# A streaming encoder step whose last output projection is computed in rows of frames

## The reference, cut to what matters

```python
SEQ, DEC_SEQ, D_MODEL, D_FF = 512, 32, 1024, 2816     # 544 frames in all
def rms_norm(x, g):
    y = xf * lax.rsqrt(jnp.mean(xf * xf, axis=-1, keepdims=True) + EPS)
    return (y * g).astype(x.dtype)
def swiglu(h, w_in, w_out):
    gu = h @ w_in
    return (jax.nn.silu(gu[..., :D_FF]) * gu[..., D_FF:]) @ w_out
for layer in range(2):
    xp = rms_norm(hp, g[0]);  mp = mixer(xp)            # layer 0: gating + attention, layer 1: pooling
    hp = hp + rms_norm(mp, g[1])
    hp = hp + rms_norm(swiglu(rms_norm(hp, g[2]), ffn_w_in[layer], ffn_w_out[layer]), g[3])
```

## Time and profile before

| | us |
|---|---|
| median of 3 runs | 1025.32 (1025.29 to 1025.61) |
| the profiled execution's own time | 1024.44 |
| its span in the trace | 1022.6 |
| PE busy | 1009.1 (99%) |
| DVE busy | 628.7 (61%) |
| ACT busy | 523.5 (51%) |
| POOL busy | 47.4 (5%) |
| HBM read | 157.46 MB, 157 GB/s over the span |

### The profile page before, as it was taken

One profiled execution on the slowest core, in us unless ns is written; L12 is line 12 of the kernel. 1 busy time (PEld: TensorE's weight loads), 2 busy tenths in 40 slices (PEclk: granted clock), 3 DMA queues, 4 the chain that ended last, 5 costly groups with the idle time before them and its releaser, 6 DMA issues.

```text
span 1022.6 us, 19108 instructions
## 1 busy us (share of the span) xinstructions
PE 1009.1 (99%) x7908; PEld 991.7 (97%) x7908; DVE 628.7 (61%) x928; ACT 523.5 (51%) x919; POOL 47.4 (5%) x55
## 2 busy tenths in 40 slices
PE   7999999999999999999999999999999999999997
PEld 6799899999999999999999999999999999999997
DVE  5396555877555555545479777899655555444643
ACT  6633666555444444444457665775544444444552
POOL 0081210000000000000000000001000000000000
PEclk9999999999999999999999999999999999999999
DMA  8322131666665555546654586556655555555554
GB/s 281 84 76 79 55 97 51 188 191 184 187 183 169 165 165 165 166 131 184 183 168 145 156 218 175 161 168 190 184 166 165 166 164 150 154 164 163 155 166 148
DMA packets 307431, 161.29 MB, mean 158 GB/s; under 512 B 14666, under 2 KB 304306, under 8 KB 307344
## 3 DMA queue, kind: packets, MB, share of 16 engines
q1 hardware_dynamic: 306880, 159.61, 53.8%
q0 software_dynamic: 224, 0.35, 0.1%
q10 hardware_dynamic: 240, 0.10, 0.0%
HBM read 157.46 MB, written 2.58 MB: 157 GB/s over the span
## 4 chain that ended last, share of the span: by engine, by line
PE 90%; DVE 6%; ACT 2%; issue 1%; DMA 1%; SPq 0%; DVEq 0%; ACTq 0%
PE ps L556 29%; PE ps L558 28%; PE ps L557 28%; DVE wlo L1528 2%; DVE tmp L1804 1%; DMA x_tok<-in_x_prompt_dram 1%; PE ps L823 1%; PE ps L809 1%; PE ps L753 0%; PE ps L644 0%; DVE acc L1764 0%; ACT whi L1085 0%; PE ps L735 0%; DVE odd_a L1922 0%; DMA raw<-in_ffn_w_out_dram 0%
## 5 line engine op out<-in xcount | busy, mean ns | idle before, releaser
L1528 DVE TENSOR_TENSOR wlo<-raw,whi 128x1024 fp32r<-128x1024 f32 (+2 forms) x332 | 367.8, 1110 | 259.8 <-ACT whi L1085 259.6
L556 PE MATMUL ps<-xhi,whi 128*128 128x256 f32 (+1 forms) x1600 | 466.6, 292 | 0.7 <-DVE wlo L1528 0.5
L558 PE MATMUL ps<-xhi,wlo 128*128 128x256 f32 (+1 forms) x1600 | 460.8, 288 | 0.0
L557 PE MATMUL ps<-xlo,whi 128*128 128x256 f32 (+1 forms) x1600 | 459.9, 287 | 0.0
L1085 ACT ACTIVATE whi<-raw 128x1024 fp32r<-128x1024 f32 (+2 forms) x332 | 316.0, 954 | 225.7 <-PE ps L558 194.3
L556 PEld LDWEIGHTS ps<-xhi,whi 128*128 128x128 f32 x1600 | 300.9, 188 | 3.2 <-issue 1.3
L557 PEld LDWEIGHTS ps<-xlo,whi 128*128 128x128 f32 x1600 | 301.1, 188 | 0.0
L558 PEld LDWEIGHTS ps<-xhi,wlo 128*128 128x128 f32 x1600 | 300.9, 188 | 0.0
L556 PE MATMUL ps<-mhi_b,whi 128*128 128x288 f32 x352 | 104.7, 297 | 0.0
L558 PE MATMUL ps<-mhi_b,wlo 128*128 128x288 f32 x352 | 104.3, 296 | 0.0
L557 PE MATMUL ps<-mlo_b,whi 128*128 128x288 f32 x352 | 102.7, 292 | 0.0
(11 more groups left out here) (231 smaller groups left out, 901.6 us busy)
## 6 DMA issues: line engine op xcount, KB each, us to landing
raw<-in_ffn_w_in_dram SPq DMA_DIRECT2D x176, 512.0 KB, 3.9
raw<-in_ffn_w_out_dram SPq DMA_DIRECT2D x64, 384.0 KB, 3.2
raw<-in_ffn_w_out_dram SPq DMA_DIRECT2D x64, 320.0 KB, 2.9
raw<-in_ab_w_in_dram SPq DMA_DIRECT2D x10, 512.0 KB, 4.7
raw<-in_ab_w_out_dram SPq DMA_DIRECT2D x10, 256.0 KB, 2.8
raw<-in_ab_w_out_dram SPq DMA_DIRECT2D x20, 128.0 KB, 3.2
x_tok<-in_x_prompt_dram SPq DMA_DIRECT2D x4, 512.0 KB, 7.8
raw<-in_ab_w_in_dram SPq DMA_DIRECT2D x8, 256.0 KB, 4.1
```

What stands on the lines that cost most here:

```text
L556: pe.matmul(out, wh, xh, start=first, stop=False)
L557: pe.matmul(out, wh, xl, start=False, stop=False)
L558: return pe.matmul(out, wl, xh, start=False, stop=last)
L1528: dve.tensor_tensor(wlo[:, s, 0:n], raw[:, m % NRAW, 0:n], whi[:, s, 0:n].bitcast(F32), ALU.subtract)\
```

## The change

**The last pass.** `ffn_out(1, 0)` becomes `rows_out`. Now 128 frames of `mhi`/`mlo` sit in the array and 512 weight columns stream, so that the result stands in rows of frames. The pass has 22 units of 2 chunks by 512 columns (each 1024 columns, 512 KB): 11 for the left half of the features, 11 for the right. In each unit PE makes 6 products for frames 0 to 127 and 6 for frames 128 to 255. The last two units are reordered: both for the first frames, then both for the second.

**The post-norm.** ACT squares each [128, 512] piece with a running sum along the row (`accum_out`), so no matmul adds squares. DVE multiplies by the gain, which lies along the row now (`g_row`, 512 KB loaded by a broadcast at unit 8). The left half's two pieces are squared and scaled at slot 11, the right half's at the end; then one root, one inversion and two multiply-adds for each 128 frames. `turn_z`, `sums_last`, the two filler matmuls and the last block's own evacuation are gone. The side work of the pass has new slots.

**The spreads.** `spread` and `spread_first` now use transposes of the broadcast column instead of matmuls with the identity; the third tile of part 1 is spread at full width and overwritten where the second belongs.

**The start.** The first half of `turn_first(1)` moves from before `va_block(0, 0)` to after it, so all 8 transposes of tile 1 stand together.

```diff
-TURN_BEFORE = {(0, 1): (1, (1,)), (1, 0): (2,), (0, 2): (3,), (0, 3): (4,)}
+TURN_BEFORE = {(0, 1): (1,), (1, 0): (2,), (0, 2): (3,), (0, 3): (4,)}
...
-    (3, 1): {"sum": 1, "spread": 2, "scale": (2, 4, 6, 8), "rows": (11, 11, 13, 13, 15, 15)},
-    (3, 0): {"h_rows": (2, 3, 5, 6), "z_rows": (18, 19), "z_more": 29},
+    (3, 1): {"sum": 1, "spread": 2, "scale": (2, 3, 4, 6), "rows": (8, 8, 9, 9, 10, 10)},
+    (3, 0): {"h_rows": (2, 3, 4, 5), "half": 11, "load": 8},
...
+FO_UNITS = {(layer, b): FC if (layer, b) == (1, 0) else 4 * KC for layer in range(2) for b in range(2)}
...
+                elif unit[0] == "fo" and unit[1:3] == (1, 0):
+                    half, i = divmod(unit[3], FC // 2)
+                    src = ffn_w_out[1].rearrange("(c p) n -> p c n", p=P)[:, 2 * i:2 * i + 2, 512 * half:512 * (half + 1)]
+                    dst = tiles(m).rearrange("p (c n) -> p c n", c=2)
...
+                if UNITS[m] == ("fo", 1, 0, STAGE[3, 0]["load"]):
+                    sp.wait_ge(w_used, FO_PASS[1, 1][-1] + 1)
+                    sp.dma_start(g_row[:, :], norm_g[1, 3].partition_broadcast(P)).then_inc(g_row_loaded, 16)
...
-            for half in range(2):
-                for t in range(2):
-                    sp.wait_ge(y_ready[t], half + 1)
-                    cols = slice(512 * half, 512 * (half + 1))
+            for t in range(2):
+                for n, cols in enumerate((slice(0, 512), slice(512, 1024))):
+                    sp.wait_ge(y_ready[t], n + 1)
...
-                    lhs, rhs = rstd[0:w, t:t + 1].broadcast_to([w, P]), ident[0:w, 0:w]
-                    mm = pe.matmul(flat(6, P + t0, w), lhs, rhs, start=True, stop=True)
+                    mm = pe.transpose(flat(6, P + t0, w), rstd[0:w, t:t + 1].broadcast_to([w, P]), ident[0:w, 0:w])
...
-            turn_first(1, (0,))
...
-                for i, t in enumerate(POOL_ROWS[b]):
+                for i, t in reversed(tuple(enumerate(POOL_ROWS[b]))):
                     w = TILES[t][1]
-                    lhs = rs[:, 3 * b + i:3 * b + i + 1].broadcast_to([P, P])
-                    mm = pe.matmul(flat(6 + b, P + i * P, w), lhs, ident[:, P - w:P], start=True, stop=True)
+                    factor = rs[:, 3 * b + i:3 * b + i + 1].broadcast_to([P, P])
+                    mm = pe.transpose(flat(6 + b, (i + 1) * P - (P - w), P), factor, ident[:, :])
...
-            def turn_z(t, ds):
-
-                for d in ds:
-                    mm = pe.transpose(flat(4 * (d // 4) + t, d % 4 * P, P), z[:, d, t * P:(t + 1) * P], ident[:, :])
-                return mm
-
-            def sums_last(squares, first):
-
-                for i in range(2):
-                    mm = pe.matmul(flat(6 + i, 0, 1), squares[:, i * P:(i + 1) * P], ones[:, :], start=first, stop=not first)
-                return mm
+            def rows_out(run):
+
+                pe.wait_ge(up_mult, inner(1, 1, FC - 1) + 1)
+                pe.wait_ge(m_lo, inner(1, 0, FC - 1) + 1)
+
+                def unit(m, t):
+                    half, i = divmod(UNITS[m][3], FC // 2)
+                    s, rows = m % NSPLIT, slice(t * P, (t + 1) * P)
+                    for c in range(2):
+                        w = slice(512 * c, 512 * (c + 1))
+                        mm = product(flat((2, 0)[half] + t, 0, 512), mhi[0][:, 2 * i + c, rows], mlo[0][:, 2 * i + c, rows],
+                                     whi[:, s, w], wlo[:, s, w], i + c == 0, 2 * i + c == FC - 1)
+                    return mm
+
+                for slot, m in enumerate(FO_PASS[1, 0]):
+                    n = UNITS[m][3]
+                    pe.wait_ge(w_lo, m + 1)
+                    if n == FC // 2:
+                        pe.wait_ge(h_rows_kept, 4)
+                    if n < FC - 2:
+                        for t in range(2):
+                            mm = unit(m, t)
+                        mm.then_inc(w_used, 1)
+                    elif n == FC - 2:
+                        unit(m, 0)
+                    else:
+                        unit(m, 0).then_inc(rows_done, 1)
+                        unit(m - 1, 1)
+                        unit(m, 1).then_inc(rows_done, 1)
+                    run(slot)
...
-                for t, slot in enumerate(STAGE[3, 0]["z_rows"]):
-                    yield slot
-                    pe.wait_ge(h_rows_kept, 4)
-                    pe.wait_ge(z_out[0], z_count(3, 3))
-                    turn_z(t, range(4)).then_inc(z_rows_turned, 1)
-                yield STAGE[3, 0]["z_more"]
-                pe.wait_ge(z_out[0], z_count(3, 6))
-                pe.wait_ge(y_ready[3], 2)
-                pe.wait_ge(y_ready[4], 2)
-                for t in range(2):
-                    turn_z(t, range(4, 7))
-                pe.wait_ge(z_added[0], add_count(3, KC - 2))
-                pe.wait_ge(rstd_done[0], 6)
-                sums_last(acc[:, 0, :], True)
...
-            ffn_out(1, 0, stepper(last_half()))
-            pe.wait_ge(r_kept[1], KEPT[3, 0])
-            fill(FILL_TAIL, 2)
-            pe.wait_ge(z_out[0], z_count(3, KC - 1))
-            sums_last(tmp2[:, (KC - 1) % 2, :], False).then_inc(sq_summed[0], 1)
-            pe.wait_ge(z_last, 1)
-            for t in range(2):
-                turn_z(t, range(7, 8)).then_inc(z_rows_turned, 1)
+            rows_out(stepper(last_half()))
...
-            def evacuate_last(d):
-
-                src = flat(out_bank(1, 0, d), 0, CUT)
-                act.wait_ge(z_added[0], add_count(3, d - 2))
-                act.activation(tmp2[:, d % 2, frames(0)], src, ACT.Square).then_inc(z_out[0], 1)
-                act.activation(z[:, d, frames(0)], src, ACT.Copy, scale=gain(1, 3, d)).then_inc(z_last, 1)
+            def square_rows(half, t):
+
+                n = 2 * half + t
+                if half:
+                    act.wait_ge(rows_done, t + 1)
+                else:
+                    act.wait_ge(w_used, AT["fo", 1, 0, FC // 2 - 1] + 1)
+                    act.wait_ge(z_added[1], add_count(3, KC - 1))
+                act.activation(tmp2[:, t, 0:512], flat((2, 0)[half] + t, 0, 512), ACT.Square,
+                               accum_out=row_sq[:, n:n + 1]).then_inc(rows_squared, 1)
+
+            def root_rows(t):
+
+                act.wait_ge(rows_squared, 3 + t)
+                act.wait_ge(rows_biased, 1)
+                act.activation(ms[:, t:t + 1], row_sq[:, 2 + t:3 + t], ACT.Sqrt, scale=1.0 / D,
+                               bias=row_bias[:, t:t + 1]).then_inc(rooted[0], 1)
+
+            def rows_out(run):
+
+                for slot, m in enumerate(FO_PASS[1, 0]):
+                    run(slot)
+                    if m + 4 < len(UNITS):
+                        hi_part(m + 4)
+                    run(slot + LATER)
...
+                yield STAGE[3, 0]["half"]
+                square_rows(0, 0)
+                square_rows(0, 1)
...
-            act.wait_ge(sq_summed[0], stat_count(3, 0))
-            act.activation(ms[:, 0:2].unsqueeze(2), ps[:, 6 * 512:8 * 512].rearrange("p (k n) -> p k n", k=2)[:, :, 0:1], ACT.Sqrt, bias=eps[:, :]).then_inc(rooted[0], 1)
+            rows_out(stepper(last_half()))
+            for t in range(2):
+                square_rows(1, t)
+                root_rows(t)
...
-            invert(3, 0, 0)
-            dve.wait_ge(rstd_done[0], stat_count(3, 0))
-            dve.wait_ge(h_rows_kept, 4)
-            for half in range(2):
-                for t in range(2):
-                    dve.wait_ge(z_rows_turned, 2 * half + t + 1)
+            def scale_rows(half, t):
+
+                cols = slice(512 * half, 512 * (half + 1))
+                dve.wait_ge(rows_squared, 2 * half + t + 1)
+                dve.wait_ge(g_row_loaded, 16)
+                dve.tensor_tensor(z_rows[:, t, cols], flat((2, 0)[half] + t, 0, 512), g_row[:, cols], ALU.mult)\
+                    .then_inc(z_rows_scaled, 1)
+
+            def last_half():
+
+                yield from norms(3, 1, 0)
+                yield STAGE[3, 0]["half"]
+                scale_rows(0, 0)
+                scale_rows(0, 1)
+                dve.tensor_scalar(row_bias[:, :], row_sq[:, 0:2], 1.0 / D, EPS, ALU.mult, ALU.add).then_inc(rows_biased, 1)
+
+            def rows_out(run):
+
+                for slot, m in enumerate(FO_PASS[1, 0]):
+                    run(slot)
+                    if m + 4 < len(UNITS):
+                        lo_part(m + 4)
+
+            rows_out(stepper(last_half()))
+            for t in range(2):
+                scale_rows(1, t)
+                dve.wait_ge(rooted[0], ROOTS[3, 0, 0] + t)
+                dve.reciprocal(rs[:, t:t + 1], ms[:, t:t + 1]).then_inc(rstd_done[0], 1)
+                dve.wait_ge(rstd_done[0], stat_count(3, 0) + t)
+                dve.wait_ge(h_rows_kept, 4)
+                for half in range(2):
+                    dve.wait_ge(z_rows_scaled, (t + 1, t + 3)[half])
                     y = y_a[:, t, 512 * half:512 * (half + 1)]
```

(36 more changed lines are left out.)

## The result

The changed kernel takes 1017.44 us (median of 4 runs, 1017.24 to 1020.63) against 1025.3 before (4 runs), a ratio of 0.9931 (95%: 0.9916 to 0.9947). Run again unchanged it took 1017.4 against 1025.17, ratio 0.9928 (0.9915 to 0.994). The forecast was 1015.8 in a range of 1013.8 to 1018.4: sign and range hold, and the gain is 7.9 us (7.8 in the second set) instead of 9.5.

What follows compares the result with a forecast made beforehand. PE's queue was taken to bound the kernel. Gains of 2.35 + 1.99 + 3.1 + 0.9 + 1.2 = 9.5 us from 1024.44 gave 1014.9, plus 0.88 to the median: 1015.8 us, range 1013.8 to 1018.4.

Steps and rivals of the forecast that it cites:

- What bounds the kernel: Whole kernel: PE's queue is the path nearly everywhere, PE busy 99% of the span, longest later wait 0.8 us.
- the slower rivals: Last pass: weight supply binds, 1032 us, chance 0.02; or PE's clock falls, 1044 for half the pass, chance 0.02.
- Streaming of the last pass, "264 x 0.231 = 61.01": Last pass: 264 products of 512 columns at the value projection's step replace 528 of 256 columns, gain 2.35 us.
- The sentence that what is saved is what each product adds: Last pass: columns streamed stay the same, only each product's added time is saved, 0.240 against 0.231 us.
- The width rival: Last pass: 512-column products have overhead of their own, step 0.240, the 2.35 us go, 1018.2 us; chance 0.08.
- Transposes of z, 1.99: Last pass: two places of four transposes, and six with the first sums, leave PE's stream; gain 1.99 us.
- The spreads, 3.1 + 0.9: Norm spreads: one transpose per tile replaces two PE instructions, gain 3.1 us; the first spread of all gains 0.9 us.
- "the chains behind it take the time up": Spreads: one reason given for a rival in which they give nothing, 4.0 us lost, 1019.8 us; chance 0.08.
- The tail, 1.2: After PE's last product to the span's end: 5.86 us instead of 7.05, gain 1.2 us, bounds 0.5 and 1.6.
- Start order, at nothing: Start: moving tile 1's first four transposes costs or gains nothing, bounds 0.3 us either way.
- Sum: Whole kernel: 2.35 + 1.99 + 3.1 + 0.9 + 1.2 = 9.5 us gained.
- From profile to median: Whole kernel: the median lies 0.88 us above the profiled execution, so 1014.9 becomes 1015.8 us.

Runs made afterwards that it cites:

- experiments 6 to 8: Changed kernel, last pass's sitting operands all from `xhi`, only `mhi_a`, or only `mlo_a` (outputs differ): 1017.54, 1019.13 and 1017.99 us, one run each.
- experiment 5: Changed kernel, right half of the last pass in 256-column products in two banks, half its columns left out of the output: 1019.58 us, one run.
- experiments 2 and 3: Changed kernel with both spreads as matmuls again: 1021.01 us; the kernel before with both spreads as transposes: 1021.98 us.
- experiment 4: Changed kernel with the first four transposes of tile 1 ahead of the first value block again: 1017.78 us.
- experiments 7 and 8: Changed kernel, last pass's sitting operands both from `mhi_a`, or both from `mlo_a` (outputs differ): 1019.13 and 1017.99 us, one run each.
- experiment 9: Changed kernel with the side work of the pre-norm at the end of layer 1's pooling one slot later: 1023.32 us, ratio 0.9983 to before.

## Why the prediction was right, and where it was 1.6 us too low

- **What bounds the kernel**: right. PE's own queue stayed the path; neither of the slower rivals appeared. Loads landed in 4.4 us, and no wait and no slower step shows in the last pass.
- **Streaming of the last pass, "264 x 0.231 = 61.01"**: the mis-sized term. The form was that of the value projection, but the step measured is 0.2343, and 264 x 0.003 is 0.8 us. The operand that sits makes most of it: with `xhi` the step is 0.2321 and the pass 0.5 us shorter (experiments 6 to 8). What makes the rest, 0.2321 against the value projection's 0.2312, is open. The gain is 264 x 0.0057 = 1.5 us instead of 2.35, half from the width and half from changing which operand sits (experiment 5). The sentence that what is saved is what each product adds holds for the first half only. The width rival (step 0.240, no gain) was wrong as well; the truth lies between.
- **Transposes of z, 1.99**: right as far as it shows. The pass is 3.81 us shorter, against 4.59 forecast, and the step explains 0.8, all of the difference.
- **The spreads, 3.1 + 0.9**: price right, cover missed. A transpose of a broadcast column costs what one of data does, 0.33 for three. They give 2.5 to 3.6 us (experiments 2 and 3). The first spread gives 0.6 of it, since PE needs 0.80 to get through five transposes and back to products, and not 0.55. In the middle 2.85 was forecast and 1.2 to 2.3 came, since 0.9 to 1.2 us come back as longer waits for DVE. The text said that the chain behind a spread starts earlier, and had "the chains behind it take the time up" only as a rival that leaves nothing; it did not ask what arrives late at the next meeting point.
- **The tail, 1.2**: 1.4 to 1.5 measured. ACT's square and accumulator read overlap a little, 0.72 from start to the root's start for 0.80; from the gain multiplication's start to the multiply-adds are 0.79 for 0.90.
- **Start order, at nothing**: right (experiment 4). The profiled run reached the first spread 1.92 us later than that of before, and so did one with the old order, at 42.74.
- **Sum**: by the table, before against changed again and without the start, the first spread gave 0.63 us (0.9 forecast), the middle 2.12 (2.85), the last pass 3.81 (4.59) and the tail 1.4 (1.2): 8.0 instead of 9.5. The medians say 7.8 and 7.9.
- **From profile to median**: the prediction added 0.88 to its sum, before's median over its profiled execution. For the changed kernel the profiled execution lies 3.2 above the median. An offset of this size is the execution's own and no part of the kernel.

No version tried that gives the whole output is faster than the changed kernel.

## What to carry to other kernels

A step read from the trace held here for its form and for the tensors it read; take it from rows with the same sitting tensor, or keep 1 to 2% of it in the range (0.2343 for 0.2312 here). Where PE is the path as here, a [128, 128] spread of a column is cheaper as a transpose (0.11 us) than as a float32 matmul (0.19 to 0.22), but count what the shorter queue runs into: the engine that feeds the next meeting point gives part of it back. A reordering of the last two units so that one chain is through before the next begins was worth 0.7 us in the tail by the profile, for no extra work.

## What the runs showed of the hardware that was not expected

- In the last pass products of the same form step by 0.2343 us with `mhi_a` or `mlo_a` sitting, in every profiled execution, and by 0.2321 with `xhi` (one execution).
- The first value block steps by 0.43 in some executions and 0.23 in others with the same code, while the windows over it show a granted clock of 1.00. So the clock's row did not account for that time, and what does is open.
- The granted clock fell to 0.50 for about 3.4 us after a PE wait of 1.5 us in one execution; the same wait in experiments 7 and 8 left it at 1.00. In experiment 9 it fell at the end of 4.7 us of waiting. What decides between the two is open.
